# A hybrid HGRN2 and dilated-attention block on one core: the attention masks added by VectorE instead of TensorE, exponentials one slot later, weighted products two units behind

## What is computed

```python
def dilated_window_attention(q, k, v, window, dilation):
    ...
    s = jnp.einsum('brhcqe,brhcke->brhcqk', qb, kb) * (E ** -0.5)
    valid = (dist >= 0) & (dist <= n) & (c * n - n + j >= 0)
    s = jnp.where(valid, s, -jnp.inf)
    m = jnp.max(s, axis=-1)
    p = jnp.exp(s - m[..., None])
    l = jnp.sum(p, axis=-1)
    o = jnp.einsum('brhcqk,brhcke->brhcqe', p, vb)
    ...
```

## Time and profile before

| | |
|---|---|
| median of 3 runs | 1445.87 us (1445.69 to 1446.19) |
| the profiled execution | 1445.46 us |
| its span, first to last instruction | 1443.7 us |
| PE busy | 1424.2 us, 99% of the span |
| PEld, DVE, ACT, POOL busy | 84%, 65%, 45%, 2% |
| a middle call, e.g. from 892 to 1040 us | about 148 us |
| the last call's attention work | 1185 to 1222.5 us |

### The profile page before, as it was taken

How to read it: one execution, slowest core, us unless ns; L and a number is a source line. 1 busy time by engine, 2 the same in 40 slices (tenths; PEclk the granted TensorE clock), 3 DMA queues, 4 the chain that set the end, 5 groups by cost and what they waited for, 6 DMA issues and landing times. The chain is left out here.

```text
span 1443.7 us, 21777 instructions
## 1 busy us (share of the span) xinstructions
PE 1424.2 (99%) x7604; PEld 1210.8 (84%) x7604; DVE 939.5 (65%) x1603; ACT 650.7 (45%) x985; POOL 34.9 (2%) x39
## 2 busy tenths in 40 slices
PE   7999999999999999999999999999999999999998
PEld 5888888888888888888888888888888889888987
DVE  7887768686868677778834784467536866544423
ACT  5355555555555555546333453344345356212211
POOL 0200000000000000013100000000000000000000
PEclk9999999999999999999999999999999999999999
DMA  5211211212121212334222222221222233333602
GB/s 210 90 44 59 74 59 61 72 58 73 58 73 51 80 44 73 115 104 111 79 76 59 59 59 86 67 56 55 94 59 59 59 113 116 138 116 118 248 30 88
DMA packets 37495, 120.59 MB, mean 84 GB/s; under 512 B 6248, under 2 KB 6568, under 8 KB 37416
## 3 DMA queue, kind: packets, MB, share of 16 engines
q1 hardware_dynamic: 37424, 119.61, 25.6%
HBM read 84.79 MB, written 22.12 MB: 74 GB/s over the span
## 5 line engine op out<-in xcount | busy, mean ns | idle before, releaser
L822 PE MATMUL z_ps<-h_hi,w_hi 128*128 128x512 f32 x704 | 279.0, 396 | 1.8 <-issue 1.3
L824 PE MATMUL z_ps<-h_hi,w_lo 128*128 128x512 f32 x704 | 274.7, 390 | 0.0
L823 PE MATMUL z_ps<-h_lo,w_hi 128*128 128x512 f32 x704 | 274.3, 390 | 0.0
L822 PEld LDWEIGHTS z_ps<-h_hi,w_hi 128*128 128x128 f32 x704 | 132.3, 188 | 28.3 <-issue 2.9
L824 PEld LDWEIGHTS z_ps<-h_hi,w_lo 128*128 128x128 f32 x704 | 132.1, 188 | 28.4
L823 PEld LDWEIGHTS z_ps<-h_lo,w_hi 128*128 128x128 f32 x704 | 132.4, 188 | 25.1
L1814 DVE TENSOR_TENSOR w_lo<-mix,w_hi 128x512 fp32r<-128x512 f32 x84 | 56.2, 690 | 92.7 <-ACT w_hi L1322 92.4
L1734 DVE TENSOR_TENSOR w_lo<-w_stage,w_hi 128x1024 fp32r<-128x1024 f32 x45 | 55.0, 1223 | 76.8 <-ACT w_hi L1244 76.6
L1507 ACT ACTIVATE pt<-pb 128x512 f32<-128x512 f32 (+1 forms) x80 | 43.5, 543 | 119.5 <-PE pb L1055 119.1
L860 PE MATMUL z_ps<-h_hi,w_hi 128*128 128x512 f32 x224 | 91.6, 409 | 0.0
L862 PE MATMUL z_ps<-h_hi,w_lo 128*128 128x512 f32 x224 | 88.0, 393 | 0.0
(11 more groups left out here) (328 smaller groups left out, 3263.4 us busy)
## 6 DMA issues: line engine op xcount, KB each, us to landing
w_stage<-w_in SPq DMA_DIRECT2D x44, 512.0 KB, 3.6
raw<-w_in SPq DMA_DIRECT2D x44, 512.0 KB, 3.5
z_swap<-zz SPq DMA_DIRECT2D x96, 128.0 KB, 2.3
gate_d<-gate SPq DMA_DIRECT2D x15, 512.0 KB, 3.1
x_in<-x SPq DMA_DIRECT2D x8, 512.0 KB, 7.5
o_a_d<-o_a SPq DMA_DIRECT2D x8, 512.0 KB, 5.1
w_stage<-w_a SPq DMA_DIRECT2D x8, 512.0 KB, 4.2
cos_t<-gate_d SPq DMA_DIRECT2D x8, 512.0 KB, 4.9
```

Of the source, the lines that this page charges most:

```text
L822: nc.tensor.matmul(z_ps[hf][:], w_hi[s][:, k, :], h_hi[:, k, t], start=k == 0, stop=False)
L823: nc.tensor.matmul(z_ps[hf][:], w_hi[s][:, k, :], h_lo[:, k, t], start=False, stop=False)
L824: last = nc.tensor.matmul(z_ps[hf][:], w_lo[s][:, k, :], h_hi[:, k, t], start=False, stop=k == KT - 1)
```

## The change

The mask matmul and its bf16 identity are gone. In a unit of group 0 or 1 the first score matmul of each region now opens it (`start=True`), in group 2 the only one does. DVE gets a new function, `add_mask`, which waits for a unit's scores and adds the mask to them in the PSUM bank; it stands first in DVE's slot, for the units that PE scored one slot earlier. ACT waits for DVE's result (`masked`) instead of PE's, and takes the exponentials of a slot's units one slot later, at the same place inside the slot as before. `weighted` follows two units behind instead of one, with a third buffer `pt2`. The table of slots is now two units in each slot from 1 to 10; `SUM_SLOTS` and `SUM_AFTER` are as before.

```diff
@@ constants and placement
-        ident_b = place("ident_b", [P, P], bf16)
...
+        pt.append(place("pt2", [P, HALF]))
...
-        UNIT_SLOTS = {1: (0,), 2: (1, 2, 3), 3: (4, 5), 4: (6, 7), 5: (8, 9), 6: (10, 11), 7: (12, 13), 8: (14, 15),
-                      9: (16, 17), 10: (18, 19)}
+        UNIT_SLOTS = {slot: (2 * slot - 2, 2 * slot - 1) for slot in range(1, 11)}
@@ PE, scores_t
-                bank = pb[:, u % 2, 0:cols]
...
-                nc.tensor.matmul(bank, ident_b[:], mask, start=True, stop=False)
                 for blk, at, n in units:
...
                     if g < 2:
-                        nc.tensor.matmul(dst, k_two[g][h][:, ks], q_two[g][h][:, qs], start=False, stop=False)
-                    last = nc.tensor.matmul(dst, k_sh[g][h][:, ks], q_sh[g][h][:, qs], start=False, stop=blk == units[-1][0])
+                        nc.tensor.matmul(dst, k_two[g][h][:, ks], q_two[g][h][:, qs], start=True, stop=False)
+                    last = nc.tensor.matmul(dst, k_sh[g][h][:, ks], q_sh[g][h][:, qs], start=g == 2, stop=True)
@@ PE, weighted and attention
-                                                pt[u % 2][:, at + P * q:at + P * q + P], start=opens, stop=closes)
+                                                pt[u % 3][:, at + P * q:at + P * q + P], start=opens, stop=closes)
...
                             scores_t(i, u)
-                            if u:
-                                weighted(i, u - 1)
+                            if u >= 2:
+                                weighted(i, u - 2)
                         if slot == 11:
+                            weighted(i, N_UNITS - 2)
                             weighted(i, N_UNITS - 1)
@@ ACT, unit_exps
-                for u in UNIT_SLOTS.get(slot, ()):
-                    act.wait_ge(st_made, (i - 1) * N_UNITS + u + 1)
+                for u in UNIT_SLOTS.get(slot - 1, ()):
+                    act.wait_ge(masked, (i - 1) * N_UNITS + u + 1)
                     cols = sum(P * k for _, _, k in unit_keys(UNITS[u][0], UNITS[u][2]))
-                    if u >= 2:
-                        act.wait_ge(pu_made, (i - 1) * N_UNITS + u - 1)
-                    nc.scalar.activation(pt[u % 2][:, 0:cols], pb[:, u % 2, 0:cols], ACT.Exp).then_inc(pt_done, 1)
+                    if u >= 3:
+                        act.wait_ge(pu_made, (i - 1) * N_UNITS + u - 2)
+                    nc.scalar.activation(pt[u % 3][:, 0:cols], pb[:, u % 2, 0:cols], ACT.Exp).then_inc(pt_done, 1)
@@ DVE
+            def add_mask(i, u):
...
+                dve.wait_ge(st_made, made)
+                scored = pb[:, u % 2, 0:cols]
...
+                nc.vector.tensor_tensor(scored, scored, mask, ALU.add).then_inc(masked, 1)
...
                     if prev:
+                        for u in UNIT_SLOTS.get(slot - 1, ()):
+                            add_mask(i, u)
                         for k in SUM_SLOTS.get(slot, ()):
```

More of the change, by code:

```diff
@@ L309, in build @@
         m_stored, m_loaded, mj_done, shift_done = sem("m_stored"), sem("m_loaded"), sem("mj_done"), sem("shift_done")
-        st_made, pt_done, pu_made = sem("st_made"), sem("pt_done"), sem("pu_made")
+        st_made, masked, pt_done, pu_made = sem("st_made"), sem("masked"), sem("pt_done"), sem("pu_made")
         ob_taken = sem("ob_taken")
@@ L348, in build @@
         ROPE_STEPS = 16
-        MASKS = 9
+        MASKS = 8
         PADS = 17
@@ L712, in _ @@
             nc.gpsimd.tensor_copy(mask_b[:], mask_in[:, 0:5, :].rearrange("p a b -> p (a b)")).then_inc(mask_done, 1)
-            nc.gpsimd.tensor_copy(ident_b[:], ident[:]).then_inc(mask_done, 1)
             pool.wait_ge(pv_made, HEADS)
@@ L1044, in scores_t @@
                 units = unit_keys(g, m)
-                cols = sum(P * n for _, _, n in units)
-                bank = pb[:, u % 2, 0:cols]
-                twice = lambda ap, n: ap.rearrange("p (a c) -> p a c", a=1).to_broadcast([P, n, ap.shape[1]])
-                mask = twice(mask_b[:, 3 * P:4 * P], 4) if g == 2 else mask_b[:, 0:cols] if cols == 3 * P else twice(mask_b[:, 0:2 * P], 2)
-                nc.tensor.matmul(bank, ident_b[:], mask, start=True, stop=False)
                 for blk, at, n in units:
@@ L2069, in link @@
                 dve.wait_ge(rope_step, steps[0])
+            def add_mask(i, u):
+                g, h, m = UNITS[u]
+                units = unit_keys(g, m)
+                cols = sum(P * n for _, _, n in units)
+                made = value(dve, (i - 1) * N_UNITS + u + 1)
+                dve.wait_ge(mask_done, MASKS)
+                dve.wait_ge(st_made, made)
+                scored = pb[:, u % 2, 0:cols]
+                if cols == 3 * P:
+                    mask = mask_b[:, 0:cols]
+                else:
+                    part_of = mask_b[:, 3 * P:4 * P] if g == 2 else mask_b[:, 0:2 * P]
+                    n = cols // part_of.shape[1]
+                    scored = scored.rearrange("p (a c) -> p a c", a=n)
+                    mask = part_of.rearrange("p (a c) -> p a c", a=1).to_broadcast([P, n, part_of.shape[1]])
+                nc.vector.tensor_tensor(scored, scored, mask, ALU.add).then_inc(masked, 1)
             def turn_count(s):
```

## The result

| | before | changed |
|---|---|---|
| median | 1445.78 us (4 runs) | 1466.17 us (4 runs, 1465.39 to 1468.23) |
| ratio | | 1.0142 (1.0130 to 1.0155) |
| profiled execution, its span | 1445.46, 1443.7 us | 1466.18, 1464.4 us |
| three middle calls and what stands before them: last projection matmul | 1184.83 us | 1204.40 us, 19.6 later |
| the last call's attention work, from there to slot 12 | 37.65 us | 38.84 us, 1.2 longer |

What follows compares the result with a forecast made beforehand. PE's own list of matmuls was taken to bound the attention; +17.7 us for three middle calls and +1.3 for the last, on the profiled 1445.46, gave 1464.5 us, range 1453 to 1474.

Steps and rivals of the forecast that it cites:

- PE bounds, any wait costs its length: Whole attention: only PE's own matmul list sets the time; removed matmuls return their slots, any PE wait costs its full length.
- Removal, 3.8 a call: 80 mask matmuls gone from PE, priced by spacing (0.22 and 0.16 us each): 3.8 us a call, 15.2 in all.
- The estimate of 10.5: Alternative gain from removing mask matmuls, by the skill's 131 ns steady spacing: at most some 10.5 us; the forecast kept 15.2.
- Odd slots, 1.33 to 1.44 each: Slots 3, 5, 7, 9: PE's scores wait for exponentials behind ACT's eviction, 1.44 or 1.33 us each, 5.5 a middle call.
- Slots 10 and 11, 0.7 + 3.1: DVE's sums 8 and 10 wait for same-slot products, delaying row maxima and evictions: PE loses 0.7 and 3.1 us a middle call.
- Slot 12, 0.35: Slot 11's rotation and slot 12's sums follow later, so PE waits again for row maxima: 0.35 us a middle call.
- Middle calls 17.7: Net loss of the three middle calls, +5.9 us each from the gain and the waits: +17.7 us.
- last call 1.3: Last call, no projection to hide behind: waits at the start and in slots 9 to 11 outweigh removed masks, +1.3 us.
- Rival 1: Only the odd slots count, DVE being in time in slots 10 to 12: 1456.3 us, chance 0.22.
- Rival 2: DVE is the bound, a mask addition costing 1.09 us: 3 to 4 us more a call, 1476 us, chance 0.11.
- Rival 3: Granted clock falls after the new waits, slowing a projection over 5 us, once per call: 1480 us, chance 0.05.
- the place that the prediction called the likeliest: PE's reckoned 2.9 us wait in the last call, where by the skill's idleness rule a clock fall was likeliest.

Runs made afterwards that it cites:

- E3: Changed kernel with both the edits of E1 and E2: 1435.30 us, ratio 0.9927 to the kernel before.
- E4: Kernel before with the 80 mask matmuls left out and nothing in their place, so no masks applied: 1431.89 us, ratio 0.9900.
- E1: Changed kernel with ACT's exponentials in odd slots put ahead of that slot's eviction, as in even slots: 1452.46 us, ratio 1.0046.
- E5: Changed kernel with masks back on TensorE and no mask additions on DVE, slots and two-unit distance kept: 1476.15 us, ratio 1.0210.
- E7: E3 with last call's first ACT rounding behind exponentials of units 0 and 1, and middle-call slots 4 and 8 taking own masks and exponentials: 1431.28 us.
- E2: Changed kernel with DVE's sums 8 and 10 (behind units 16 and 18) one slot later: 1454.08 us, ratio 1.0052.
- E8: Changed kernel with each mask addition on DVE done twice, one behind the other: 1474.12 us, ratio 1.0195.

## Why the prediction was right, step by step

- **PE bounds, any wait costs its length.** Held in the main: the slots add up to 18.7 of the 19.6 us, and the other 0.9 lies before the attention. But PE was not quite free of waits before. Against E3 the kernel before has 0.6 us too many in slot 12 and 0.35 in slot 14 of a call, which the list of waits does not show.
- **Removal, 3.8 a call.** Method right (spacing, not duration): the slots show it. What comes out is 14.1 us (E4), since 1.1 of it turns into waits for exponentials that the matmuls had covered. The estimate of 10.5 that the prediction made from the Trainium skill (TensorE: Matmul & The Clock Gate, section "Back-to-back issue gap") was further off.
- **Odd slots, 1.33 to 1.44 each.** Seen: 1.44 over the unhindered length in slot 3 (9.42 against E4's 7.98), 1.40 in slot 7 against E1's 7.72. PE starts at T + 1.56 where I had T + 1.57. E1 and E5 show that the place of the exponentials is the cause. What the forecast did not see is that slots 5 and 9 have a second reason behind the first (the copies of q), which E7 took away.
- **Slots 10 and 11, 0.7 + 3.1.** Right in mechanism, confirmed by E2; the sizes were 1.0 (10.52 against E3's 9.51) and 3.7 (11.44 against E3's 7.73). The wait for the product was 1.59 to my 1.7, the maxima came 1.35 late as reckoned, and the restarts took the rest.
- **Slot 12, 0.35.** Wrong: it got 0.13 shorter. PE came later to its maxima by as much as DVE did, and PE had waited there before the change already (1.09 against 0.62 us for the four maxima, under E2).
- **Middle calls 17.7, measured 18.7; last call 1.3, measured 1.2.** That the sum comes so near is in part luck, since errors cancel. Over E4's slots a middle call has 5.1 us more in the odd slots 3 to 9 (forecast 5.5), 1.0 in slot 10 (0.7), 3.4 in slot 11 once product 18's own 0.89 is taken off (3.1) and -0.1 in slot 12 (0.35), and the masks give back 3.4 (3.8). In the last call the wait at the start was 2.59 us to the 2.9 reckoned, and slots 9 and 11 waited 1.1 and 1.7 to 1.25 and 1.85.
- **Rival 1** (1456.3) is in effect what E2 built: 1454.1. **Rival 2** fell by E8 and by the 696 ns row. **Rival 3** is not what made this result, but it is no empty rival. In the profiled execution of the changed kernel the granted clock stayed at 1.00 (2.4 GHz) over PE's longest wait, 2.59 us at the start of the last call. In E1 a wait of the same length at the same place was followed by a stretch at 0.50 (1.2 GHz). First the changed kernel, then E1; in the rows of stretches stand us, busy times of PE, PEld, DVE, ACT and POOL with counts, then PEclk:

```profile
1208.33 0.38 PE L1047 MATMUL pb<-q_two,k_two 128*128 128x256 f32 x1 [2.59 <-ACT pt L1501]
1205.00:1210.00 5.00, 2.41 (x21) 2.21 (x20) 3.12 (x4) 4.77 (x7) 0.00 (x0) 1.00 0.66 231
```

```profile
1193.21 0.58 PE L1047 MATMUL pb<-q_two,k_two 128*128 128x256 f32 x1 [2.59 <-ACT pt L1501]
1193.20:1195.80 2.60, 2.59 (x13) 2.59 (x13) 0.70 (x1) 1.91 (x3) 0.00 (x0) 0.50 0.97 389
```

The same work, from that matmul to the scores of unit 4, takes 2.74 us in the changed kernel and 4.32 in E1: the fall costs 1.6 us. E2 has it too, behind a wait of 2.20 us (0.50 from 1195.50 to 1198.70), and E3's profile, with 2.59 us again, has not. So it comes in some executions and not in others. Of E3's four, three have a mean granted clock of 1.000 and 1434.2 to 1435.3 us, the fourth 0.998 and 1437.55; the slowest execution of the changed kernel, 1468.23 us, has the lowest clock of its four, 0.997. A mean does not say where the clock fell, so for these executions it is a likely reading, not a shown one. What decides between the two is open. No profile here shows a fall in a middle call, behind waits of up to 1.6 us, so the 5 us a call of rival 3 did not come. Its price was not read from a lower clock either: the profile gives 1.00 for the stretch of the earlier trace rows as well. The page's row of granted clock can't show any of this, since a slice of it is some 36 us long; E1's reads 9 throughout.

The Trainium skill's rule that the prediction named in that place (TensorE: Matmul & The Clock Gate, section "What's actually happening") is that idleness brings the array back to 1.2 GHz. The traces of E1 and E2 agree with it, at the place that the prediction called the likeliest, and those of the changed kernel and E3 show that such a wait need not do it.

## What to carry to other kernels

When a step is moved one slot later on one engine, look at what stands before it there in every kind of slot: the same distance in slots was harmless in the even ones and cost 1.4 us in each odd one, because the eviction ahead of it waits for the very work that the freed bank is wanted behind. Check too that each consumer whose producer was moved has moved with it; two sums left in their old slots cost 12 us, and 17 once the exponentials stood right (E1 against E3). With both set right (E3), and then the copies of q passed (E7), the changed order with the masks on VectorE is 15 us faster than the kernel before. Not all of that is the masks: some 3 us are the old waits for row maxima in slots 12 and 14, which the later sums took away. Whether later sums alone would bring them in the kernel before was not run.

## What the runs showed of the hardware

- Adding to a PSUM bank in place on DVE (696 ns for 512 columns, 564 for 384) costs about as much as PSUM to SBUF (690), as the prediction had taken.
- Behind a wait of PE of 2.2 to 2.6 us the granted clock fell from 1.00 to 0.50 in the profiles of E1, E2 and E8 and stayed at 1.00 in those of the changed kernel and E3. A fall cost 1.6 us in E1. Of E3's four executions the one with the lower mean clock took 2.2 us more than the next.
